# Expert down weights fetched as whole rows, and pair weights in two products

## The reference

```python
y = jnp.zeros_like(hf)
for e in range(N_EXPERTS):                                  # 16
    a = jax.nn.silu(hf @ w_gate[e]) * (hf @ w_up[e])        # 256x1024 @ 1024x512, twice
    y = y + comb_dense[:, e:e + 1] * (a @ w_down[e])        # 256x512 @ 512x1024
```

## Time and profile before

| | us |
|---|---|
| median of three executions | 506.24 |
| span of the profiled execution, first to last instruction | 504.1 |
| TensorE busy | 489.8 |
| expert stage in the profile, first product to last (L1926 to L1913) | 281.8 to 496.1 |
| data moved over the span | 149.28 MB, 296 GB/s |
| data moved, page's slices 25 to 38 | 399 to 409 GB/s |

### The profile page before, as it was taken

One profiled execution on the slowest core, in us unless ns is written; L12 is line 12 of the kernel. 1 busy time (PEld: TensorE's weight loads), 2 busy tenths in 40 slices (PEclk: granted clock), 3 DMA queues, 4 the chain that ended last, 5 costly groups with the idle time before them and its releaser, 6 DMA issues.

```text
span 504.1 us, 7151 instructions
## 1 busy us (share of the span) xinstructions
PE 489.8 (97%) x2784; PEld 333.7 (66%) x2784; DVE 249.4 (49%) x469; ACT 196.6 (39%) x353; POOL 15.7 (3%) x30
## 2 busy tenths in 40 slices
PE   8999999999999999999999999999999999999993
PEld 8998998788888888878998534433443344433331
DVE  3764787988788689976664621111111111111113
ACT  5464667557626555345674211111211121111113
POOL 2000000000120000000100000000000000000000
PEclk9999999999999999999999999999999999999998
DMA  7797675543456448986799799999999999999992
GB/s 254 240 324 212 206 236 182 167 151 114 129 172 202 155 132 226 381 309 210 280 406 402 279 409 403 399 400 400 403 404 400 399 400 405 403 401 399 399 364 89
DMA packets 68026, 149.28 MB, mean 296 GB/s; under 512 B 8790, under 2 KB 15124, under 8 KB 67988
## 3 DMA queue, kind: packets, MB, share of 16 engines
q1 hardware_dynamic: 67684, 148.24, 81.0%
q10 hardware_dynamic: 304, 0.53, 0.3%
HBM read 147.69 MB, written 1.05 MB: 295 GB/s over the span
## 4 chain that ended last, share of the span: by engine, by line
PE 51%; issue 45%; DVE 2%; ACT 1%; POOL 0%; POOLq 0%; DVEq 0%; ACTq 0%
PE bank L1480 14%; PE bank L1481 14%; PE bank L1482 14%; PE bank L1487 2%; PE bank L1503 1%; PE bank L1591 1%; PE bank L1614 1%; PE bank L1587 1%; DVE al L957 1%; PE bank L1753 0%; PE bank L1736 0%; ACT ah L593 0%; PE bank L1776 0%; PE bank L1705 0%; PE bank L1745 0%
## 5 line engine op out<-in xcount | busy, mean ns | idle before, releaser
L971 DVE TENSOR_TENSOR wl<-raw,wh 128x1024 fp32r<-128x1024 f32 (+1 forms) x80 | 94.2, 1197 | 31.8 <-ACT wh L593 30.2
L593 ACT ACTIVATE wh<-raw 128x1024 fp32r<-128x1024 f32 (+1 forms) x80 | 81.5, 1041 | 55.7 <-PE bank L1482 40.3
L1480 PE MATMUL bank<-wh,ah 128*128 128x512 f32 (+2 forms) x248 | 95.1, 384 | 0.8 <-issue 0.8
L1481 PE MATMUL bank<-wl,ah 128*128 128x512 f32 (+2 forms) x248 | 93.3, 376 | 0.0
L1482 PE MATMUL bank<-wh,al 128*128 128x512 f32 (+2 forms) x248 | 93.3, 376 | 0.0
L1480 PEld LDWEIGHTS bank<-wh,ah 128*128 128x128 f32 x248 | 46.7, 188 | 9.3 <-issue 1.3
L1482 PEld LDWEIGHTS bank<-wh,al 128*128 128x128 f32 x248 | 46.6, 188 | 8.6
L1481 PEld LDWEIGHTS bank<-wl,ah 128*128 128x128 f32 x248 | 46.7, 188 | 7.8
L1480 PE MATMUL bank<-ah,wh 128*128 128x256 f32 x160 | 45.6, 285 | 0.6 <-DVE wl L971 0.4
L1481 PE MATMUL bank<-al,wh 128*128 128x256 f32 x160 | 45.3, 283 | 0.0
L1482 PE MATMUL bank<-ah,wl 128*128 128x256 f32 x160 | 45.3, 283 | 0.0
(11 more groups left out here) (372 smaller groups left out, 910.1 us busy)
## 6 DMA issues: line engine op xcount, KB each, us to landing
raw<-in_w_in SPq DMA_DIRECT2D x48, 512.0 KB, 5.0
wh_raw<-in_w_exp_up SPq DMA_DIRECT2D x13, 512.0 KB, 12.3
raw<-in_w_branch SPq DMA_DIRECT2D x12, 512.0 KB, 4.2
wl_raw<-in_w_exp_gate SPq DMA_DIRECT2D x12, 512.0 KB, 11.3
gates<-in_w_exp_gate SPq DMA_DIRECT2D x11, 512.0 KB, 11.1
raw<-in_w_exp_up SPq DMA_DIRECT2D x11, 512.0 KB, 12.5
gates<-in_w_exp_down SPq DMA_DIRECT2D x10, 512.0 KB, 10.6
gates<-in_w_exp_up SPq DMA_DIRECT2D x9, 512.0 KB, 11.1
```

Of the source, the lines that this page charges most:

```text
L593: act.activation(dst, src, ACT.Copy, scale=scale).then_inc(done, 1)
L971: dve.tensor_tensor(wl[:, n % RING, 0:sz], raw[:, n % RING, 0:sz], wh[:, n % RING, 0:sz].bitcast(F32), ALU.subtract)\
L1480: pe.matmul(dst, st[0], mv[0], start=start, stop=False, skip_group_check=True)
L1481: pe.matmul(dst, st[0], mv[1], start=False, stop=False, skip_group_check=True)
```

## The change

The down weights of pairs 0 to 6 come as four units `rows` (pair, kt). Each has, for both experts, rows 128 kt to 128 kt + 127 of the down weights with all 1024 columns: 512 KB in one stretch of memory, one piece of 4 KB for each partition. All four are issued and waited for in the even step n = 2p+2. `down_rows(dst, p, half)` does the products of one column half, in the same order as before; the second half is done in step 2p+3 from the same four units. A counter of its own, `rows_spent`, rises five times for each pair: once after the first half, and once after each kt of the second. The place of a `rows` unit is free when the second half has used it. The last pair keeps its two times two down units, and the loop for the rest of the rows keeps its own units.

In `sel_T`, four products with 64 stationary columns and one moving column become two with 128 stationary columns and two moving columns; ScalarE picks the two halves with two instructions of 64 x 1 in place of one of 128 x 1. Semaphores of the early stages are put together (`consts_set`, `early_T`, `small_exp`, `gains_in`), with the waits moved to the right counts.

```diff
@@ expert_units
-        if n >= lag:
+        if lag <= n and (n - lag) // 2 < PAIRS - 1 and n % 2 == 0:
+            out += [("rows", (n - lag) // 2, kt) for kt in range(4)]
+        if (n - lag) // 2 == PAIRS - 1:
             out += [("down", n - lag, j) for j in range(2)]
...
+SINGLE = [u for u in UNITS if u[0] != "rows"]
+FAST = len(SINGLE)
+ROWS_OF_PAIR = 5
...
+        def used_up(u):
+
+            kind, n, j = UNITS[u]
+            if kind == "rows":
+                return rows_spent, ROWS_OF_PAIR * n + 1 + j + 1
+            return spent, SINGLE.index((kind, n, j)) + 1
...
-                if what == "down":
+                if what == "rows":
+                    src = a["w_exp_down"][0, 2 * n + c % 2][P * j:P * j + P, :]
+                elif what == "down":
...
-                    sp.wait_ge(spent, chunks[at - RAWX] // 2 + 1)
+                    sp.wait_ge(*used_up(chunks[at - RAWX] // 2))
...
@@ sel_cols, on ScalarE
-                act.activation(combs[:, p % 2:p % 2 + 1], bank[2][:, 256:257], ACT.Copy).then_inc(s_("combs_ready"), 1)
+                for i, r in enumerate(row_half):
+                    ins = act.activation(combs[r, p % 2:p % 2 + 1], bank[2][r, 256 + i:257 + i], ACT.Copy)
+                ins.then_inc(s_("combs_ready"), 1)
...
-                if 2 <= n <= EXPERTS:
-                    y_hi(p, bank[1], p + 1, UNIT["down", n - 2, 1] + 1)
+                if 2 <= n < EXPERTS:
+                    y_hi(p, bank[1], p + 1, rows_spent, ROWS_OF_PAIR * p + (ROWS_OF_PAIR if n % 2 else 1))
+                if n == EXPERTS:
+                    y_hi(p, bank[1], p + 1, spent, SINGLE.index(("down", n - 2, 1)) + 1)
...
@@ sel_T, on TensorE
                 for t in range(T):
-                    for i in range(2):
-                        n = 2 * p + i
-                        mm = pe.matmul(bank[2][row_half[i], 256:257], sel_f32[:, g % 2, t, at + CAP * i:at + CAP * i + CAP],
-                                       weight[:, t, n:n + 1], start=(t == 0), stop=(t == T - 1), skip_group_check=True)
+                    mm = pe.matmul(bank[2][:, 256:258], sel_f32[:, g % 2, t, at:at + P], weight[:, t, 2 * p:2 * p + 2],
+                                   start=(t == 0), stop=(t == T - 1), skip_group_check=True)
...
+            def down_rows(dst, p, half):
+
+                for kt in range(4):
+                    slot, times = fill_of("rows", p, kt)
+                    pe.wait_ge(*landed(slot, times))
+                    for i in range(2):
+                        mm = pe.matmul(dst[row_half[i], :], aT[:, kt, row_half[i]], HOMES[2 * slot + i][0][:, 512 * half:512 * half + 512],
+                                       start=(kt == 0), stop=(kt == 3), skip_group_check=True)
+                    if half or kt == 3:
+                        mm.then_inc(rows_spent, 1)
...
@@ the loop over n, on TensorE
-                    for j in range(2):
-                        down(bank[1], j, fill_of("down", n - 2, j))
+                    if n < EXPERTS:
+                        down_rows(bank[1], p, n % 2)
+                    else:
+                        for j in range(2):
+                            down(bank[1], j, fill_of("down", n - 2, j))
```

More of the change, by code:

```diff
@@ L266, in program @@
         arrived_x = [sem(f"expert_unit_arrived_{s}") for s in range(RAWX // 2)]
-        spent = sem("expert_unit_spent")
+        spent, rows_spent = sem("expert_unit_spent"), sem("down_rows_spent")
         hi_done, lo_done, used = sem("hi_done"), sem("lo_done"), sem("chunk_used")
@@ L487, in _ @@
                 else:
-                    sp.wait_ge(spent, chunks[at - RAWX] // 2 + 1)
+                    sp.wait_ge(*used_up(chunks[at - RAWX] // 2))
                 load_chunk(slot, c, UNITS)
-            sp.wait_ge(spent, chunks[max(at for at in range(len(chunks)) if at % RAWX == FIN_SLOT)] // 2 + 1)
-            sp.dma_start(g_fin, a["g_final"].partition_broadcast(P)).then_inc(s_("gfinal_in"), 16)
+            sp.wait_ge(*used_up(chunks[max(at for at in range(len(chunks)) if at % RAWX == FIN_SLOT)] // 2))
+            sp.dma_start(g_fin, a["g_final"].partition_broadcast(P)).then_inc(s_("gains_in"), 16)
             sp.wait_ge(s_("overflow_ready"), 1)
@@ L494, in _ @@
             with sp.If(over > 0):
-                sp.wait_ge(spent, PASS)
+                sp.wait_ge(spent, FAST)
                 with sp.Fori(0, ROUNDS) as r:
                     for c in range(2 * PASS):
-                        sp.wait_ge(spent, r * PASS + PASS + c // 2 - RAWG // 2 + 1)
+                        sp.wait_ge(spent, r * PASS + FAST + c // 2 - RAWG // 2 + 1)
                         load_chunk(c % RAWG, c, SPILL_UNITS)
@@ L520, in _ @@
             g.affine_select(out=ident[:, :], in_=ident[:, :], compare_op=ALU.not_equal, fill=1.0, base=0,
-                            pattern=[[-1, P]], channel_multiplier=1).then_inc(s_("ident_set"), 1)
+                            pattern=[[-1, P]], channel_multiplier=1).then_inc(s_("consts_set"), 1)
             link(g.memset(half_neg, -0.5))
@@ L664, in _ @@
                     act.wait_ge(s_("rows_in"), 16 * (len(ROWS) + 3))
-                    act.activation(da[:, 0:8], a_log, ACT.Exp).then_inc(s_("a_exp"), 1)
+                    act.activation(da[:, 0:8], a_log, ACT.Exp).then_inc(s_("small_exp"), 1)
                     act.wait_ge(s_("lam_dots"), 2)
-                    act.activation(lam[:, 2:4], lam[:, 0:2], ACT.Exp).then_inc(s_("lam_exp"), 1)
+                    act.activation(lam[:, 2:4], lam[:, 0:2], ACT.Exp).then_inc(s_("small_exp"), 1)
                 if name == "q":
@@ L681, in _ @@
                     act.wait_ge(s_("dt_arg"), 1)
-                    act.activation(sp_e, sp_z, ACT.Exp, scale=-1.0).then_inc(s_("dt_exp"), 1)
+                    act.activation(sp_e, sp_z, ACT.Exp, scale=-1.0).then_inc(s_("small_exp"), 1)
                 if n == FIRST["bcd"] + 1:
-                    act.wait_ge(s_("consts_set"), 1)
+                    act.wait_ge(s_("consts_set"), 2)
                     act.activation(flip_r[:, :], flip[:, :], ACT.Copy).then_inc(s_("toep_ready"), 1)
@@ L689, in _ @@
                 if n == LAST["bcd"] + 1:
-                    act.wait_ge(s_("early_T"), 2)
+                    act.wait_ge(s_("early_T"), 3)
                     act.activation(xr[:, 4:6, TAPS - 1:], pT[:, :].rearrange("p (k n) -> p k n", k=2), ACT.Copy)\
@@ L852, in silu, with y_hi @@
                 act.activation(act_pair[n // 2 % 2][row_half[n % 2], :], src[r, :], ACT.Silu).then_inc(s_("gate_silu"), 1)
-            def y_hi(p, src, weights, units):
+            def y_hi(p, src, weights, done, units):
                 act.wait_ge(s_("combs_ready"), weights)
-                act.wait_ge(spent, units)
+                act.wait_ge(done, units)
                 act.activation(yh[:, :], src[:, :], ACT.Copy, scale=combs[:, p % 2:p % 2 + 1]).then_inc(s_("y_hi"), 1)
@@ L862, in y_last_hi @@
                     if j:
-                        act.wait_ge(spent, PASS)
+                        act.wait_ge(spent, FAST)
                     else:
@@ L876, in _ @@
                 if n < EXPERTS:
-                    silu(gate_bank(n), n, UNIT["gu", n, 3] + 1)
+                    silu(gate_bank(n), n, SINGLE.index(("gu", n, 3)) + 1)
                 if e >= 2 and g + 1 < GROUPS:
@@ L898, in _ @@
                             for half in range(2):
-                                y_hi(p, bank[1], r * PAIRS + PAIRS + p + 1, r * PASS + PASS + 12 * p + 8 + 2 * half + 2)
+                                y_hi(p, bank[1], r * PAIRS + PAIRS + p + 1, spent, r * PASS + FAST + 12 * p + 8 + 2 * half + 2)
                 act.wait_ge(s_("scatter_pe"), T * EXPERTS * (ROUNDS + 1))
@@ L943, in _ @@
                 if t == 0:
-                    dve.wait_ge(s_("g_cols_pe"), 1)
+                    dve.wait_ge(s_("early_T"), 1)
                     dve.tensor_copy(g_cols[:, :], bank[0][:, 0:KD]).then_inc(s_("g_cols_ready"), 1)
@@ L992, in softplus_begin @@
             def softplus_begin():
-                dve.wait_ge(s_("dt_exp"), 1)
+                dve.wait_ge(s_("small_exp"), 3)
                 link(dve.tensor_scalar(sp_q, sp_e, 2.0, None, ALU.add))
@@ L1075, in _ @@
                 if n == LAST["k"] + 1:
-                    dve.wait_ge(s_("early_T"), 1)
+                    dve.wait_ge(s_("early_T"), 2)
                     dve.tensor_copy(vecT[:, :], pO[:, 0:50]).then_inc(s_("vecT_ready"), 1)
                 if n == 5:
-                    dve.wait_ge(s_("consts_set"), 1)
+                    dve.wait_ge(s_("consts_set"), 2)
                     link(dve.tensor_copy(iota, ints[:, 0:P]))
@@ L1461, in gained @@
                 dve.tensor_tensor(hm[:, t, c], bank[4 + 2 * t + half][:, :], g_fin[:, c], ALU.mult).then_inc(s_("gained_rows"), 1)
-            dve.wait_ge(s_("gfinal_in"), 16)
+            dve.wait_ge(s_("gains_in"), 32)
             gained(0, 0)
@@ L1487, in keep_warm @@
```

(11 more changed lines are left out.)

8 lines of the change are left out of this document (4 added, 4 removed).

## The result

The changed kernel takes 517.89 us in the median (517.73 to 518.69, four runs), the kernel before 506.29 (505.99 to 506.44) beside it. The ratio is 1.0232, 95% interval 1.0217 to 1.0246: 11.6 us slower, where 11.5 were forecast (517.8).

What follows compares the result with a forecast made beforehand. TensorE was taken to bound the expert stage, the stream leading by 1.0 us. A late last gate/up chunk (11.6) plus `sel_T` (0.1) took the 504.1 span to 515.8; with 2.1 around it, less 0.1, 517.8 us; range 513 to 520.5.

Steps and rivals of the forecast that it cites:

- What bounds the kernel: Expert stage: TensorE bounds it, the DMA engines are full too, and the weight stream leads by 1.0 us at the end.
- Part 1, pieces: Weight stream: 4 KB pieces save 0.06 us for each of 56 chunks, 3.4 us of stream, none of it TensorE's time.
- Part 2, order: Odd expert's gate/up units stand two units (5.1 us) later; without a dry spell, expert 15's last chunk lands 1.1 us late.
- Part 3, the hold: SP's wait for pair 0's rows place, freed after step 3's second half: next issue at 327.0, 13.4 us later.
- Restart: DMA stream after the queue runs dry: 5.3 us from SP's issue to the first landing, at 332.3.
- The dry spell: DMA queue empty after the landing at 320.5 until SP issues at 327.0: costs 10.5 us of stream.
- The deciding chunk: Last chunk of expert 15's gate/up: lands at 487.2, 121 intervals of 1.28 us after 332.3; TensorE 11.6 us late.
- One hole and not seven: Later rows places, pair 1's onward: 7.7 us of work on the way against 5.3 for a restart, so no further dry spell.
- Part 4, `sel_T`: New pair-weight products on TensorE: +0.11 us a pair, only pair 7's counting, +0.1; bounds for eight pairs -1.3 to +0.9.
- Part 5, semaphores: Early stages' semaphores put together: no cost, within 0.3 us either way.
- two signs: TensorE's gate/up waits for DMAs in steps 11 to 15, about 11 us in all, and granted clock 1.00 there.
- Rival (b), the clock: Late gate/up units leave TensorE idle, its clock falls to 1.2 GHz over expert 15's units: 522 us; chance 0.06.

Runs made afterwards that it cites:

- The kernel with the wait alone: Kernel before plus one SP wait: the chunk issued at 313.61 waits until step 3's first down unit is used up; 517.46 us, ratio 1.0205.
- the kernel with pieces alone: Kernel before, down units of pairs 0 to 6 reading whole rows in 4 KB pieces, old order and waits; 506.00 us, ratio 0.9988.
- the kernel with pairs 2 to 6: Changed kernel, but pairs 0 and 1 keep their old down units and order; 508.50 us, ratio 1.0037.
- 2 to 5: Changed kernel, but only pairs 2 to 5 come as whole rows, the others in old units and order; 506.27 us, ratio 0.9988.
- The edit of step 3: Changed kernel, in step 3 alone scatter and pair 0's second half moved behind the second of four gate/up units; 512.44 us, ratio 1.0104.
- the list without pair 0: Changed kernel, but pair 0 keeps its old down units, pairs 1 to 6 as whole rows; 511.58 us, ratio 1.0097.

## Why the prediction was right

The mechanism was right. That the number met the median within 0.1 us is partly luck: a term that was 1.4 us too high and a pace that was 1.2 us too quick over the 121 intervals cancel.

**What bounds the kernel: right.** Both limits were full and the lead was 1.0 us. The kernel with the wait alone and the kernel with pieces alone bear this out from both sides: a delay of the stream is time, a gain of it is not.

**Part 1, pieces: right in kind, small in size.** Forecast 1.28 us for a chunk of 4 KB pieces; from 330.9 to 487.0 it is 1.29 over 121 intervals, 1.2 us more in all.

**Part 2, order: right, and sized a little low.** Forecast 1.1 us late without the hole; the kernel with pairs 2 to 6, which has no hole, is 2.2 slower than that with 2 to 5. With the measured pace, 319.9 + 122 x 1.29 = 477.3, 1.7 late.

**Part 3, the hold: right, step by step.** SP's issue 327.0, measured 326.97. Last landing before it 320.5, measured 319.9. Restart 5.3 us after the issue, measured 3.9: this term was 1.4 too high. It had been worked back from the fifth chunk behind the gap of before, but these chunks were not issued all at once (the third at 284.86, the fourth at 286.15). The first of them gives the term directly (issue and time to landing, in the kernel before):

```profile
L419 SPq DMA_DIRECT2D x<-in_w_exp_down x1: 379/379/379, 283.9 to 283.9; - x1
...
DMA to landing us min/median/max: 4.1/4.1/4.1
```

With 4.1 the forecast would have been 516.6. The dry spell was 10.5, measured 330.9 - 319.9 - 1.3 = 9.7. The deciding chunk 487.2, measured 487.0: the quick restart and the slower pace cancel, so the total is better than its terms. One hole and not seven: right. That it is the ring's turn is shown by the added wait, which changes nothing else. The edit of step 3 and the list without pair 0 agree; they also move products, or change pair 0's pieces and order.

**Part 4, `sel_T`: wrong in sign.** +0.11 a pair was taken, and the trace has -0.06, within the bounds given. The products themselves are 0.03 us longer, and what precedes them is 0.09 shorter, which the forecast had not priced. Whether that is the change from 128 to 64 stationary columns behind the transposes is not shown by a run of its own. As forecast, it hides in the changed kernel.

**Part 5, semaphores: nothing was taken, and no run isolates them.** The kernel with pairs 2 to 5 has them, the new `sel_T` and four pairs in whole rows, and is at 0.9988, so together they cost nothing that can be measured.

**What would show it: two signs came out otherwise.** The hole, SP's silence and the rate are as foretold. TensorE's waits for data up to the deciding unit are 8.2 us (from 315.16 to 487.18, 172.02 us with 163.78 busy), not 11: 1.4 us of its lateness is the half clock below, and a wait is shown some 0.16 us shorter than it is, as records are drawn 0.59 us long at a distance of 0.43 and the last one before a wait covers its start. And the granted clock was not 1.00 throughout.

**Rival (b), the clock: it happened and cost nothing in the main runs.** TensorE ran most of expert 15's first unit at 0.86 us for a pair of records instead of 0.43. The section "HAM oscillation — how this bites in real kernels" of the Trainium skill's "TensorE: Matmul & The Clock Gate" tells of a fall at each wait for a DMA, in a kernel whose waits it gives as some 3 to 5 us. Here the waits are 0.3 to 1.6 us, and the traces have one fall of 3.4 us among nine idle stretches of 0.3 us or more ahead of that unit, behind two of the three longest (1.5 and 1.6 us, with 1.1 us of products between); in the other steps the clock stayed at 1.00. The lost time was inside the waits for the next landings: TensorE still idled for 0.62 us before the unit that decides, and started it 0.2 us after its landing. It is not free in every case: in the changed kernel with the old `sel_T` the clock stands at 0.62 over 9 us, the deciding chunk lands at 486.7, and its unit starts at 487.36:

```profile
478.00:487.00 9.00, 7.83 (x24) 2.68 (x26) 0.75 (x1) 0.41 (x1) 0.00 (x0) 0.62 1.03 404
```

That is 0.7 us behind the landing instead of 0.2, with no idle time before it: a loss of some 0.5 us, of the kind that (b) described at an eighth of its size.

## What to carry to other kernels

Where two limits both look full, find the lead of one over the other at the end. It says which changes cost time, and which gains are not seen. When a buffer in an in-order ring is used twice, price the later release at the place of the issuing queue: the time of the new release against the landing of the last transfer that was issued before it. Here the same hold cost 6.7, 3.1 and 0 us at three turns of the ring, by what was still on the way when it began. Work that is moved to release a buffer early may be the cover of another wait. And where a measured row gives a term directly, take it rather than work it back from a later one.

## What the runs showed of the hardware

A DMA queue that has run dry is back 3.6 to 4.3 us after the next issue, by the first landing of a 512 KB chunk: 3.6 to 3.9 in six kernels with 4 KB pieces (3.9 in the changed one), 4.1 and 4.3 with 2 KB pieces (the kernel before at 284 us, the added wait). A stream of 512 KB chunks passes at 407 to 411 GB/s in 4 KB pieces, 390 in 2 KB ones. The granted clock fell to half behind idle stretches of TensorE of 1.5 and 1.6 us with 1.1 us of products between. It stayed at 1.00 behind stretches of 1.1 and 1.6 us with as much between (the edit of step 3, ahead of 474.22), and behind a row of stretches of 0.6 to 0.7 us: in the kernel with the added wait twelve such stretches pass between 446 and 486 us, most with 1.9 us of products between.
